# Scattering the experts' outputs in two passes of rounded fp32

## The chip, the cores and the metric

One Trainium2 chip, one of its cores. The metric is device time in microseconds (us) of one execution, median of three runs. TensorE is PE in the profile, VectorE is DVE, ScalarE is ACT, SyncE issues the DMAs of the weights (its queue is SPq). "fp32r" is rounded fp32: a matmul on it is one record in the trace, where a full fp32 matmul is two.

## The reference

Two layers of a hybrid backbone on 256 latent tokens (and 256 context tokens in the first layer) of width 1024. The change lies in the last stage alone, the channel mixer of layer 1, which is a top-2-of-8 mixture of SwiGLU experts:

```
def moe_swiglu(h, router, w1, w3, w2):
    logits = (h @ router).astype(jnp.float32)
    top_v, top_i = lax.top_k(logits, TOP_K)
    wts = jax.nn.softmax(top_v, axis=-1)
    comb = jnp.sum(jax.nn.one_hot(top_i, N_EXPERTS, dtype=jnp.float32) * wts[..., None], axis=-2)
    return sum(comb[..., e:e + 1].astype(h.dtype) * swiglu(h, w1[e], w3[e], w2[e])
               for e in range(N_EXPERTS))
...
        x = x + g2 * channel_mixer(h2, layer, ffn_w1, ffn_w3, ffn_w2, moe_router, moe_w1, moe_w3, moe_w2)
```

Eight experts, each with w1 and w3 of 1024x3584 and w2 of 3584x1024, all fp32. The result is the latent stream (256 x 1024).

## The kernel before, in words

All engines run programs written out by hand, with semaphores between them. Matmuls on weights use a split: a value is rounded to fp32r ("high"), the rest is kept as another fp32r ("low"), and three products (high x high, low x high, high x low) are added in PSUM.

**The expert stage.** Each expert has 128 slots. DVE ranks the tokens of each expert and writes 0/1 matrices Pm (token x slot) by comparing the rank with an iota (`select`, L1616). PE gathers: `gather` (L754 to L762) multiplies the tokens htok by Pm in full fp32. The expert's width of 3584 is worked in 14 pairs of 256 columns (PAIRS = 14). For each pair PE runs `up` (24 matmuls, 512 columns, L805 to L807), `turned` (2 transposes, L814) and `down` (12 matmuls, L826 to L828), which adds into banks 4 and 5 over the 14 pairs. ACT makes the high parts of the weights (L921, L927, L934), the silu (L1129) and the high part of the activation (L1133). DVE makes the low parts (L1269, L1275, L1282), the product (L1652) and the low part of the activation (L1656). SyncE fetches 3 pieces of 1 MB for each pair, each once the DVE instruction that reads the buffer's old contents is done.

**Scatter before.** Once, in the first expert: `select_rest` on DVE writes Pm for experts 1 to 7 and multiplies it by the token weights COMB into Pw (L1633). PE transposes Pw, 16 blocks of 128x128, in two halves (`turn_weighted`, L771 to L781, after `turned` of pair 1 and of pair 2). ACT copies them to the context half of xT (`keep_weighted`, L1112), which has no other use by then. For each expert e, at pairs 2 and 3 of the expert after it: ACT copies the sums from banks 4 and 5 to ysum (`sums`, L1124 and L1125). PE runs `scatter(e, half)`, at pair 2 with half 0 and at pair 3 with half 1, each 4 full-fp32 matmuls of 128x128 on 256 columns (L791), and DVE adds them to x with the gate (`update`, L1645, 4 instructions a half). The semaphore sums_read releases both the scatter and the next `down` that starts banks 4 and 5 anew. The last expert's scatter comes at the end, with nothing behind it but the updates and the output's DMA.

**Order around the change.** In each of an expert's pairs DVE runs: product of the pair before, act_low and down_low of the pair two before, up_b_low of the next, up_a_low of the one after, and at j = 2 and 3 `update`. PE at j = 2 runs up, turned, scatter half 0, down. At j = 3 it runs up, turned, scatter half 1, down.

Of the kernel before, what the change touches and what calls it, by code (L numbers as in the profile page):

```python
# [13 lines left out]
F32 = mybir.dt.float32  # L14
F32R = mybir.dt.float32r
# [5 lines left out]
P = 128  # L21
# [30 lines left out]
ALL_PAIRS = E * PAIRS  # L52
PIECE = 2 * D

BEFORE = {"ffn_y_free": 1, "scatter_free": 1, "up_a_used": 2, "moe_up_full": 2, "down_used": 2, "sums_read": 1}

# [65 lines left out]
def build(nc, xT_in, consts_in, pool_in, vec_in, cond_in, rows_in, router_in, first_in, mod_in, attn_in, ffn13_in, ffn2_in, moe_up_in, moe_down_in, out):  # L124
    with ExitStack() as ctx:
# [16 lines left out]
        def at(name, shape, off=None, dt=F32, parts=P):  # L142
# [5 lines left out]
            assert off + n <= room - 32, (name, off + n, room)  # L148
            return nc.alloc_sbuf_tensor_at(name, [parts, *shape], dt, offset=base + 4 * off)

        xT = at("xT", [KD, T])
        const = at("const", [CONST_LEN])
        vec = at("vec", [DEPTH, VEC_LEN])
# [99 lines left out]
        mprod = at("mprod", [2, 2 * P])  # L253
        mah = at("mact_high", [2, 2 * P], dt=F32R)
        mal = at("mact_low", [2, 2 * P], dt=F32R)
        Pw = at("Pw", [2, E, SLOTS], late)
        ysum = sg[:, :, :].rearrange("p a b -> p (a b)")

        banks = [ctx.enter_context(nc.psum_tensor(f"bank{b}", [P, 512], F32)) for b in range(8)]

# [187 lines left out]
        def _(pe):  # L448
# [315 lines left out]
            def experts(n):  # L764
# [6 lines left out]
                def turn_weighted(half):  # L771

                    if half == 0:
                        pe.wait_ge(S("weighted_ready"), n + 1)
                    else:
                        pe.wait_ge(S("turned_read"), 4 * n + 2)
                    for r in range(2 * half, 2 * half + 2):
                        for i in range(4):
                            e, t = divmod(4 * r + i, 2)
                            last = pe.transpose(banks[6 + r % 2][:, i * P:(i + 1) * P], Pw[:, t, e, :], C("ident"))  # L780
                        last.then_inc(S("turned_full"), 1)  # L781

                def scatter(e, half):

                    if half == 0:
                        pe.wait_ge(S("sums_read"), e + (n * E + 2))
                    for q in range(2 * half, 2 * half + 2):
                        pe.wait_ge(S("scatter_free"), e * 4 + (n * 4 * E + 1 + max(0, q - 1)))
                        for i in range(2):
                            k = 2 * q + i  # L790
                            last = mm(banks[6 + q % 2][:, i * LAT:(i + 1) * LAT], ysum[:, k * P:(k + 1) * P],  # L791
                                      xT[:, bass.ds(e, 1), LAT:T], start=True, stop=True)
                        last.then_inc(S("scatter_full"), 1)

                def up(g, u):
# [35 lines left out]
                def expert(e, first=False):  # L831
                    g0 = e * PAIRS + n * ALL_PAIRS
                    pe.wait_ge(S("gathered_low"), e * 2 + (n * 2 * (E + 1) + 2))
                    up(g0, 0)
                    if not first:
                        turned(g0 - 1, 1)
                        down(g0 - 2, 0)
                    up(g0 + 1, 1)
                    turned(g0, 0)
                    if not first:  # L840
                        down(g0 - 1, 1, stop=True)
                    up(g0 + 2, 0)
                    turned(g0 + 1, 1)
                    if first:
                        turn_weighted(0)
                    else:
                        scatter(e - 1, 0)
                    pe.wait_ge(S("sums_read"), e + (n * E + 1))
                    down(g0, 0, start=True)
                    up(g0 + 3, 1)  # L850
                    turned(g0 + 2, 0)
                    if first:
                        turn_weighted(1)
                    else:
                        scatter(e - 1, 1)
                    down(g0 + 1, 1)
                    with pe.Fori(2, PAIRS // 2 - 1) as q:
                        for u in range(2):
                            g = g0 + q * 2
                            up(g + u, u)  # L860
                            turned(g + (u - 1), 1 - u)
                            down(g + (u - 2), u)
                    g = g0 + (PAIRS - 2)
                    up(g, 0)
                    turned(g - 1, 1)
                    down(g - 2, 0)
                    up(g + 1, 1)
                    if first:
                        pe.wait_ge(S("turned_read"), 4 * n + 4)
                    pe.wait_ge(S("scatter_free"), e * 4 + (n * 4 * E + 1))  # L870
                    gather(e * SLOTS + SLOTS)
                    turned(g, 0)
                    down(g - 1, 1)
# [23 lines left out]
        def _(act):  # L897
# [210 lines left out]
            def experts(n):  # L1108
                def keep_weighted(half):
                    for r in range(2 * half, 2 * half + 2):  # L1110
                        act.wait_ge(S("turned_full"), n * 4 + r + 1)
                        fn(xT[:, 2 * r:2 * r + 2, LAT:T], banks[6 + r % 2][:, :].rearrange("p (e t) -> p e t", t=LAT), ACT.Copy) \  # L1112
                            .then_inc(S("turned_read"), 1)

                if n:
# [5 lines left out]
                def sums(e):  # L1121

                    act.wait_ge(S("down_used"), e * 2 * PAIRS + (2 * n * ALL_PAIRS + 2 * PAIRS + 2))
                    fn(ysum[:, 0:512], banks[4][:, :], ACT.Copy)  # L1124
                    fn(ysum[:, 512:D], banks[5][:, :], ACT.Copy).then_inc(S("sums_read"), 1)  # L1125

                def silu(g, u):
                    act.wait_ge(S("moe_up_full"), g + 3)
# [61 lines left out]
        def _(dve):  # L1190
# [417 lines left out]
            def experts(n):  # L1608
# [19 lines left out]
                def select_rest():  # L1628

                    for t in range(2):  # L1630
                        step(select(t, 1, E))
                        comb = R[:, COMB, t].unsqueeze(2).broadcast_to([P, E, SLOTS])
                        last = tt(Pw[:, t], Pm[:, t, 0:E * SLOTS].rearrange("p (e s) -> p e s", s=SLOTS), comb, ALU.mult)  # L1633
                    last.then_inc(S("weighted_ready"), 1)

                def update(e, half):

                    if half == 0:
                        dve.wait_ge(S("scatter_free"), e * 4 + (n * 4 * E + 1))
                    for q in range(2 * half, 2 * half + 2):  # L1640
                        dve.wait_ge(S("scatter_full"), e * 4 + (n * 4 * E + q + 1))
                        for i in range(2):
                            k = 2 * q + i
                            x = xT[:, k, 0:LAT]
                            last = stt(out=x, in0=banks[6 + q % 2][:, i * LAT:(i + 1) * LAT],  # L1645
                                       scalar=modT[:, 1, 5 * KD + k, 0:1], in1=x, op0=ALU.mult, op1=ALU.add)
                        last.then_inc(S("scatter_free"), 1)

                def product(g, u):

# [8 lines left out]
                def expert(e, first=False, last=False):  # L1659
                    g0 = e * PAIRS + n * ALL_PAIRS  # L1660
                    for j in range(4):
                        g, u = g0 + j, j % 2
                        if j or not first:
                            product(g - 1, 1 - u)
                        if j >= 2 or not first:
                            act_low(g - 2, u)
                            down_low(g - 2, u)
                        if first and j == 1:
                            select_rest()
                        up_b_low(g + 1, 1 - u)  # L1670
                        up_a_low(g + 2, u)
                        if j >= 2 and not first:
                            update(e - 1, j - 2)
                    with dve.Fori(2, PAIRS // 2 - 1) as q:
                        for u in range(2):
                            g = g0 + q * 2
                            product(g + (u - 1), 1 - u)
                            act_low(g + (u - 2), u)
                            down_low(g + (u - 2), u)
                            up_b_low(g + (u + 1), 1 - u)  # L1680
                            up_a_low(g + (u + 2), u)
                    for j in range(PAIRS - 2, PAIRS):
                        g, u = g0 + j, j % 2
                        product(g - 1, 1 - u)
                        act_low(g - 2, u)
                        down_low(g - 2, u)
                        if not last or j + 1 < PAIRS:
                            up_b_low(g + 1, 1 - u)
                        if not last:
                            up_a_low(g + 2, u)  # L1690
                    gathered_low(e * 2 + (n * 2 * (E + 1) + 2))
# [8 lines left out]
                down_low(g - 2, 0)  # L1700
                act_low(g - 1, 1)
                down_low(g - 1, 1)
                for half in range(2):
                    update(E - 1, half)

# [156 lines left out]
```

## Time and profile before

| what | value |
|---|---|
| time, median of 3 runs | 2235.92 us (2235.74 to 2236.14) |
| the profiled execution's own time | 2234.71 us |
| its span in the trace | 2232.9 us |
| PE busy | 2135.7 us, 96% of the span |
| DVE busy | 1713.1 us, 77% |
| ACT busy | 1120.7 us, 50% |
| DMA, mean over the span | 229 GB/s |

The profiled execution's time is its span and 1.8 us around it. Durations in the rows are those of single instructions; PE's overlap, so what one costs there is the step from one start to the next, which the chain of waits shows.

### The profile page before, as it was taken

The numbers are of one execution on the slowest core, as the hardware profiler recorded it, in microseconds if no ns is written. First come the engines' busy times: TensorE is split into PE (matmuls) and PEld (weight loads), VectorE is DVE, ScalarE is ACT, GpSimd is POOL, SyncE is SP. The second block draws the span as 40 slices with busy tenths as digits, with TensorE's granted clock in tenths as the row PEclk, the third lists the DMA queues.
The fourth block names the chain that finished last, engine by engine and source line by source line (L and its number), as shares of the span: only waits on it lengthen the run. The fifth ranks groups of instructions, "written<-read, shape, count | busy, mean of one in ns | idle before, by whom it ended". The sixth has DMA issues, their size and how long they took to land.

```text
span 2232.9 us, 27842 instructions
## 1 busy us (share of the span) xinstructions
PE 2135.7 (96%) x9866; PEld 1710.4 (77%) x9866; DVE 1713.1 (77%) x2158; ACT 1120.7 (50%) x1276; POOL 42.5 (2%) x84
## 2 busy tenths in 40 slices
PE   8989999998999999779997999999999999999997
PEld 6765776655788888667987888888888888888886
DVE  7777687646767766777745988988898988889895
ACT  3316221213333332434334777767777777767774
POOL 0000000000000000000000000000000000000000
PEclk9999999999999999899997999999999999999999
DMA  7500244343444443222444899989899999989993
GB/s 316 198 24 1 95 175 141 123 151 113 154 166 170 159 159 133 94 72 78 177 165 188 348 368 346 371 329 371 333 362 359 350 349 350 372 324 368 336 375 118
DMA packets 77284, 512.38 MB, mean 229 GB/s; under 512 B 8738, under 2 KB 9890, under 8 KB 22820
## 3 DMA queue, kind: packets, MB, share of 16 engines
q1 hardware_dynamic: 65700, 469.59, 55.9%
q0 software_dynamic: 11520, 41.95, 5.4%
q8 instruction: 38, 0.62, 0.1%
q14 instruction: 26, 0.21, 0.0%
HBM read 510.46 MB, written 1.05 MB: 229 GB/s over the span
## 4 chain that ended last, share of the span: by engine, by line
PE 88%; DVE 8%; ACT 2%; issue 2%; DMA 1%; SPq 0%; DVEq 0%; ACTq 0%
PE bank L807 9%; PE bank L805 9%; PE bank L806 9%; PE bank L556 5%; PE bank L558 5%; PE bank L557 5%; PE bank L668 5%; PE bank L826 5%; PE bank L828 5%; PE bank L827 5%; PE bank L678 4%; PE bank L724 2%; PE bank L725 2%; PE bank L726 2%; PE bank L700 2%; PE bank L710 2%
## 5 line engine op out<-in xcount | busy, mean ns | idle before, releaser
L934 ACT ACTIVATE down_high<-W 128x1024 fp32r<-128x1024 f32 x224 | 237.1, 1064 | 139.3 <-PE bank L828 139.2
L1275 DVE TENSOR_TENSOR up_b_low<-W,up_b_high 128x2048 fp32r<-128x2048 f32 x112 | 256.5, 2290 | 56.5 <-ACT up_b_high L927 56.5
L1282 DVE TENSOR_TENSOR down_low<-W,down_high 128x1024 fp32r<-128x1024 f32 x224 | 271.8, 1223 | 31.8 <-ACT down_high L934 22.5
L556 PE MATMUL bank<-h_high,tile_high 128*128 128x512 f32 (+1 forms) x704 | 259.7, 369 | 11.7 <-DVE tile_low L1326 11.7
L1269 DVE TENSOR_TENSOR up_a_low<-W,up_a_high 128x2048 fp32r<-128x2048 f32 x112 | 255.8, 2284 | 1.9 <-ACT up_a_high L921 1.9
L558 PE MATMUL bank<-h_high,tile_low 128*128 128x512 f32 (+1 forms) x704 | 239.3, 340 | 0.0
L557 PE MATMUL bank<-h_low,tile_high 128*128 128x512 f32 (+1 forms) x704 | 239.2, 340 | 0.0
L921 ACT ACTIVATE up_a_high<-W 128x2048 fp32r<-128x2048 f32 x112 | 212.9, 1901 | 2.1 <-PE bank L807 2.1
L927 ACT ACTIVATE up_b_high<-W 128x2048 fp32r<-128x2048 f32 x112 | 213.2, 1903 | 0.0
L826 PE MATMUL bank<-down_high,mact_high 128*128 128x512 f32 x448 | 186.4, 416 | 2.6 <-DVE down_low L1282 2.6
L828 PE MATMUL bank<-down_low,mact_high 128*128 128x512 f32 x448 | 176.3, 393 | 0.0
L805 PE MATMUL bank<-up_a_high,gathered_high 128*128 128x512 f32 x448 | 174.5, 390 | 1.4 <-DVE gathered_low L1603 1.4
L827 PE MATMUL bank<-down_high,mact_low 128*128 128x512 f32 x448 | 175.4, 392 | 0.0
L807 PE MATMUL bank<-up_b_low,gathered_high 128*128 128x512 f32 x448 | 175.0, 391 | 0.0
L805 PE MATMUL bank<-up_b_high,gathered_high 128*128 128x512 f32 x448 | 174.4, 389 | 0.3 <-DVE up_b_low L1275 0.3
L807 PE MATMUL bank<-up_a_low,gathered_high 128*128 128x512 f32 x448 | 174.3, 389 | 0.0
L806 PE MATMUL bank<-up_b_high,gathered_low 128*128 128x512 f32 x448 | 174.3, 389 | 0.0
L806 PE MATMUL bank<-up_a_high,gathered_low 128*128 128x512 f32 x448 | 174.3, 389 | 0.0
L556 PEld LDWEIGHTS bank<-h_high,tile_high 128*128 128x128 f32 x704 | 135.6, 193 | 35.2 <-DVE tile_low L1326 12.6
L1065 ACT ACTIVATE sg<-bank 128x512 f32<-128x512 f32 (+1 forms) x64 | 31.4, 490 | 261.2 <-PE bank L558 261.1
L557 PEld LDWEIGHTS bank<-h_low,tile_high 128*128 128x128 f32 x704 | 135.7, 193 | 21.9 <-issue 7.9
L558 PEld LDWEIGHTS bank<-h_high,tile_low 128*128 128x128 f32 x704 | 135.5, 192 | 14.7
(229 smaller groups left out, 4087.7 us busy)
## 6 DMA issues: line engine op xcount, KB each, us to landing
W<-in_moe_up SPq DMA_DIRECT2D x224, 1024.0 KB, 6.0
W<-in_moe_down SPq DMA_DIRECT2D x112, 1024.0 KB, 4.9
W<-in_w_mod_later POOLq DMA_DIRECT2D x80, 512.0 KB, 3.7
W<-in_ffn SPq DMA_DIRECT2D x33, 1024.0 KB, 4.8
W<-in_attn_blocks SPq DMA_DIRECT2D x24, 1280.0 KB, 5.9
W<-in_attn_blocks SPq DMA_DIRECT2D x22, 1024.0 KB, 5.2
W<-in_attn_blocks SPq DMA_DIRECT2D x8, 1536.0 KB, 7.1
shift_tiles<-in_w_mod_first SPq DMA_DIRECT2D x8, 512.0 KB, 13.9
```

Source lines behind the costliest of these rows:

```text
L556: mm(b[:, 0:n], wh[:, r, k, :], hh[:, k, 0:n], start=k == 0, stop=False)
L557: mm(b[:, 0:n], wh[:, r, k, :], hl[:, k, 0:n], start=False, stop=False)
L558: last = mm(b[:, 0:n], wl[:, r, k, :], hh[:, k, 0:n], start=False, stop=k == KD - 1)
L805: mm(b[:, :], hgh[:, k, :], high[u][:, kk, :], start=k == 0, stop=False)
L806: mm(b[:, :], hgl[:, k, :], high[u][:, kk, :], start=False, stop=False)
L807: last = mm(b[:, :], hgh[:, k, :], low[u][:, kk, :], start=False, stop=k == KD - 1)
L826: mm(b[:, :], mah[:, u, a], ch[:, h, w], start=start and h == 0, stop=False, skip_group_check=True)
L827: mm(b[:, :], mal[:, u, a], ch[:, h, w], start=False, stop=False, skip_group_check=True)
L828: last = mm(b[:, :], mah[:, u, a], cl[:, h, w], start=False, stop=stop and h == 1, skip_group_check=True)
L1269: tt(al[u][:], raw_a[u].rearrange("p (k n) -> p k n", k=KD // 2), ah[u][:].bitcast(F32), ALU.subtract) \
L1275: tt(bl[u][:], raw_b[u].rearrange("p (k n) -> p k n", k=KD // 2), bh[u][:].bitcast(F32), ALU.subtract) \
L1282: tt(cl[:, h, :], raw_c[u][:, h * D:(h + 1) * D], ch[:, h, :].bitcast(F32), ALU.subtract) \
```

## The change

The token weights leave the scatter matrix. What PE transposes and ACT keeps is now the 0/1 matrix Pm, kept as fp32r (PmT, at xT's address). The weight of each slot, one number for each slot and expert, is made once by 16 matmuls of Pm with one column of COMB (in `turn_weighted(0)`, into bank 7), and DVE copies it to wslot after `down_low` of pair 0, at j = 2 of the first expert; PE's transposes of r = 1 into the same bank wait for that copy. The sums of an expert are multiplied by wslot as they leave PSUM: ACT writes the high part (ysh, with a scale operand of one value a partition), and DVE, in a new function `sums_low`, the low part (ysl), before act_low at j = 2. The scatter is two fp32r matmuls on the same PSUM region instead of one full-fp32 matmul. The multiplication of Pm by COMB on DVE is gone. sums_low_ready, counted by DVE, takes the place of sums_read, counted by ACT. The gather stays as it was.

```
-        Pw = at("Pw", [2, E, SLOTS], late)
-        ysum = sg[:, :, :].rearrange("p a b -> p (a b)")
+        ysh = at("sums_high", [D], late, dt=F32R)
+        ysl = at("sums_low", [D], late + D, dt=F32R)
+        PmT = at("PmT", [KD, T], xT_at, dt=F32R)
+        wslot = sg[:, 0, 0:E]
...
                 def turn_weighted(half):
                     if half == 0:
-                        pe.wait_ge(S("weighted_ready"), n + 1)
+                        pe.wait_ge(S("rest_selected"), n + 1)
+                        for e in range(E):
+                            for t in range(2):
+                                last = mm(banks[7][:, e:e + 1], Pm[:, t, e * SLOTS:(e + 1) * SLOTS],
+                                          R[:, COMB, t, e:e + 1], start=t == 0, stop=t == 1)
+                        last.then_inc(S("slot_weights_full"), 1)
                     else:
                         pe.wait_ge(S("turned_read"), 4 * n + 2)
                     for r in range(2 * half, 2 * half + 2):
+                        if r == 1:
+                            pe.wait_ge(S("slot_weights_read"), n + 1)
                         for i in range(4):
                             e, t = divmod(4 * r + i, 2)
-                            last = pe.transpose(banks[6 + r % 2][:, i * P:(i + 1) * P], Pw[:, t, e, :], C("ident"))
+                            last = pe.transpose(banks[6 + r % 2][:, i * P:(i + 1) * P],
+                                                Pm[:, t, e * SLOTS:(e + 1) * SLOTS], C("ident"))
...
                 def scatter(e, half):
                     if half == 0:
-                        pe.wait_ge(S("sums_read"), e + (n * E + 2))
+                        pe.wait_ge(S("sums_low_ready"), e + (n * E + 2))
...
-                            last = mm(banks[6 + q % 2][:, i * LAT:(i + 1) * LAT], ysum[:, k * P:(k + 1) * P],
-                                      xT[:, bass.ds(e, 1), LAT:T], start=True, stop=True)
+                            b = banks[6 + q % 2][:, i * LAT:(i + 1) * LAT]
+                            mm(b, ysh[:, k * P:(k + 1) * P], PmT[:, bass.ds(e, 1), LAT:T], start=True, stop=False)
+                            last = mm(b, ysl[:, k * P:(k + 1) * P], PmT[:, bass.ds(e, 1), LAT:T], start=False, stop=True)
...
-                    pe.wait_ge(S("sums_read"), e + (n * E + 1))
+                    pe.wait_ge(S("sums_low_ready"), e + (n * E + 1))
                     down(g0, 0, start=True)
...
-                    fn(ysum[:, 0:512], banks[4][:, :], ACT.Copy)
-                    fn(ysum[:, 512:D], banks[5][:, :], ACT.Copy).then_inc(S("sums_read"), 1)
+                    for hf in range(2):
+                        fn(ysh[:, hf * 512:(hf + 1) * 512], banks[4 + hf][:, :], ACT.Copy, scale=wslot[:, bass.ds(e, 1)]) \
+                            .then_inc(S("sums_high_ready"), 1)
...
                 def select_rest():
                     for t in range(2):
-                        step(select(t, 1, E))
-                        comb = R[:, COMB, t].unsqueeze(2).broadcast_to([P, E, SLOTS])
-                        last = tt(Pw[:, t], Pm[:, t, 0:E * SLOTS].rearrange("p (e s) -> p e s", s=SLOTS), comb, ALU.mult)
-                    last.then_inc(S("weighted_ready"), 1)
+                        last = select(t, 1, E)
+                    last.then_inc(S("rest_selected"), 1)
...
+                def sums_low(e):
+                    for hf in range(2):
+                        dve.wait_ge(S("sums_high_ready"), e * 2 + (2 * n * E + hf + 1))
+                        a = slice(hf * 512, (hf + 1) * 512)
+                        last = stt(out=ysl[:, a], in0=banks[4 + hf][:, :], scalar=wslot[:, bass.ds(e, 1)], in1=ysh[:, a].bitcast(F32),
+                                   op0=ALU.mult, op1=ALU.subtract)
+                    last.then_inc(S("sums_low_ready"), 1)
...
                         if j >= 2 or not first:
+                            if j == 2 and not first:
+                                sums_low(e - 1)
                             act_low(g - 2, u)
                             down_low(g - 2, u)
                         if first and j == 1:
                             select_rest()
+                        if j == 2 and first:
+                            dve.wait_ge(S("slot_weights_full"), n + 1)
+                            dve.tensor_copy(wslot, banks[7][:, 0:E]).then_inc(S("slot_weights_read"), 1)
...
                 act_low(g - 1, 1)
                 down_low(g - 1, 1)
+                sums_low(E - 1)
                 for half in range(2):
                     update(E - 1, half)
```

## Rows read from the trace of the kernel before

**Rows 1.** The page: the span in 40 slices, PE busy in tenths, and its granted clock.
```profile
PE   8989999998999999779997999999999999999997
...
PEclk9999999999999999899997999999999999999999
```

**Rows 2.** Who waited for whom from 1260 to 2200: us in total, times, longest.
```profile
DVE up_b_low L1275 <- ACT up_b_high L927: 51.8, 96, 0.6
```

**Rows 3.** The chain of waits at one expert's boundary: start us, us, what.
```profile
1358.42 0.22 PE bank L814 x2
1358.63 1.73 PE bank L791 x8
1360.36 0.24 PE bank L826
...
1378.94 0.24 PE bank L826
```

**Rows 4.** The chain of waits in layer 1's projections, rounded fp32 on 256 columns.
```profile
1062.11 0.12 PE bank L558
```

**Rows 5.** Timeline of DVE at the boundary: start, us, tile, count, idle before.
```profile
1354.40 0.42 DVE L1656 TENSOR_TENSOR mact_low<-bank,mact_high 128x256 fp32r<-128x256 f32 x1 [2.10 <-ACT mact_high L1133]
1355.35 2.36 DVE L1282 TENSOR_TENSOR down_low<-W,down_high 128x1024 fp32r<-128x1024 f32 x2 [0.52 <-ACT down_high L934]
1358.10 2.29 DVE L1275 TENSOR_TENSOR up_b_low<-W,up_b_high 128x2048 fp32r<-128x2048 f32 x1 [0.39 <-ACT up_b_high L927]
...
1373.65 2.35 DVE L1282 TENSOR_TENSOR down_low<-W,down_high 128x1024 fp32r<-128x1024 f32 x2
```

**Rows 6.** Timeline of ACT there.
```profile
1353.50 0.59 ACT L1125 ACTIVATE sg<-bank 128x512 f32<-128x512 f32 x1
```

**Rows 7.** Groups of DVE and ACT by shape: count, busy us, mean ns, idle before.
```profile
L1445 DVE SCALAR_TENSOR_TENSOR conv<-ypad,vec,conv 128x512 f32<-128x512 f32 x60 | 41.7, 745 | 0.0
...
L1065 ACT ACTIVATE sg<-bank 128x512 f32<-128x512 f32 x32 | 19.1, 597 | 184.3 <-PE bank L558 184.3
...
L967 ACT ACTIVATE root<-bank,const 128x512 f32<-128x512 f32 x3 | 2.1, 687 | 11.3 <-PE bank L475 11.3
```

**Rows 8.** Two stretches, PE alone: length, busy (records), clock, DMA share, GB/s.
```profile
36.00:38.00 2.00, 2.00 (x20) 1.00 0.96 404
1205.40:1207.70 2.30, 2.26 (x10) 0.50 0.00 0
```

**Rows 9.** Timeline of DVE in the first expert, pairs 1 and 2.
```profile
1225.36 1.22 DVE L1633 TENSOR_TENSOR Pw<-Pm,R 128x1024 f32<-128x1024 f32 x1
...
1228.76 2.29 DVE L1275 TENSOR_TENSOR up_b_low<-W,up_b_high 128x2048 fp32r<-128x2048 f32 x1
...
1233.83 2.35 DVE L1282 TENSOR_TENSOR down_low<-W,down_high 128x1024 fp32r<-128x1024 f32 x2
```

**Rows 10.** Timeline of PE there: start, us, tile, idle before and its releaser.
```profile
1230.42 0.39 PE L807 MATMUL bank<-up_a_low,gathered_high 128*128 128x512 f32 x1
...
1231.10 0.50 PE L805 MATMUL bank<-up_b_high,gathered_high 128*128 128x512 f32 x1 [0.30 <-DVE up_b_low L1275]
```

**Rows 11.** The chain of waits, in the first expert and at the end.
```profile
1234.39 0.87 PE bank L780 x8
...
2219.84 0.48 ACT sg L1124
...
2220.98 1.15 PE bank L791 x4
```

**Rows 12.** Timeline of DVE at the end.
```profile
2222.22 1.67 DVE L1645 SCALAR_TENSOR_TENSOR xT<-bank,modT,xT 128x256 f32<-128x256 f32 x4 [4.23 <-PE bank L791]
2224.32 1.74 DVE L1645 SCALAR_TENSOR_TENSOR xT<-bank,modT,xT 128x256 f32<-128x256 f32 x4 [0.43 <-PE bank L791]
```

**Rows 13.** SyncE's queue from 1230 to 2200, and all DMA from 1260 to 1340.
```profile
SPq L404 <- DVE down_low L1282: 350.7, 109, 8.1
...
DMA packets 4184, 30.44 MB, mean 381 GB/s; under 512 B 469, under 2 KB 469, under 8 KB 469
```

More of the change, by code:

```diff
@@ L53 @@
 PIECE = 2 * D
-BEFORE = {"ffn_y_free": 1, "scatter_free": 1, "up_a_used": 2, "moe_up_full": 2, "down_used": 2, "sums_read": 1}
+BEFORE = {"ffn_y_free": 1, "scatter_free": 1, "up_a_used": 2, "moe_up_full": 2, "down_used": 2, "sums_low_ready": 1}
 COLS = {}
@@ L149, in at @@
             return nc.alloc_sbuf_tensor_at(name, [parts, *shape], dt, offset=base + 4 * off)
+        xT_at = top[0]
         xT = at("xT", [KD, T])
@@ L1111, in keep_weighted @@
                         act.wait_ge(S("turned_full"), n * 4 + r + 1)
-                        fn(xT[:, 2 * r:2 * r + 2, LAT:T], banks[6 + r % 2][:, :].rearrange("p (e t) -> p e t", t=LAT), ACT.Copy) \
+                        fn(PmT[:, 2 * r:2 * r + 2, LAT:T], banks[6 + r % 2][:, :].rearrange("p (e t) -> p e t", t=LAT), ACT.Copy) \
                             .then_inc(S("turned_read"), 1)
```

## The prediction

> **What bounds the kernel now.** I read the page's slices first: in the last half of the span, the expert stage, PE is busy in nine tenths or more of every slice and its granted clock stays at full speed [rows 1]. Then the waits of that stage: DVE waits 51.8 us for ACT, 96 times, at most 0.6 us each, and PE does not stand among the waiters at all [rows 2]. Last the chain of waits at one expert's boundary, where every piece is PE's [rows 3]. So between the first expert and the last one the time is the sum of PE's steps. What the change takes from PE there is worth its full length, so long as the wait that would come last next (DVE's low parts) still comes before PE. Two places are different: the first expert's early pairs, where DVE is once in the chain, and the end, where PE, ACT and DVE take turns. I take the three places one after the other, against the profiled execution (2234.71 us, of which the span is 2232.9); the median of the runs is 1.2 us above it, and the difference is carried over to the median.
>
> **Scatter on PE, experts 0 to 6 (inside the loop).** A half is 4 full-fp32 matmuls, 8 records, and takes 1.73 us of the chain [rows 3], 0.433 us a matmul. After the change it is 8 fp32r matmuls of 128x128 on 256 columns. The trace has the same shape in layer 1's projections, each with its own stationary tile too, and there the chain steps 0.12 us [rows 4]. So a half is 8 x 0.12 = 0.96 us, 0.77 us less, and 7 experts x 2 halves save 10.8 us. Bounds: at the smallest step that a 128-column record shows, 0.109 us (0.87 us for 8) [rows 11], it would be 12.0 us; at the step of today's records, 0.216 us, nothing. I take 0.12, since shape, type and change of the stationary tile are the same.
>
> **ACT's and DVE's new work at the boundary.** ACT's two copies get a scale operand. The nearest pair of rows, 128x512 without and with a one-value-a-partition operand, is 597 and 687 ns [rows 7]: +0.09 us each, 0.18 us an expert, in front of ACT's next work. DVE gets two 128x512 instructions of scalar_tensor_tensor form, 745 ns each [rows 7], 0.66 us from start to start because neighbours overlap by some 0.08: 1.4 us an expert. They stand between product and act_low at j = 2. Today DVE is idle there for 2.10 us, waiting for ACT's mact_high, which ACT makes only after its two copies [rows 5, 6]. ACT's second copy runs 1353.50 to 1354.09, and the first starts 0.49 us ahead of it; with the dearer form the first ends about 1353.70. DVE's two run 1353.75 to 1355.15, act_low follows to 1355.5, and down_low, which starts at 1355.35 today, starts at about 1355.5. Then up_b_low waits for ACT as before and moves only with ACT's 0.2 us (1358.10 to 1358.3). So the idle stretch hides nearly all of it. Behind the new wait on DVE's queue stand act_low, down_low, up_b_low, up_a_low and the updates, and SyncE's three pieces, which follow the low parts.
>
> Does PE still find its operands? The scatter's half 0 starts at 1358.63 [rows 3] and needs the second DVE instruction, done at 1355.15: 3.5 us to spare. The closest one is down of pair 2. PE starts it at 1378.94 today [rows 3], both halves of the scatter earlier that is 1.54 us sooner, 1377.4. Its down_low runs 1373.65 to 1376.0 [rows 5] and moves by 0.2 us, because DVE works without a gap from 1358.10 up to it. That leaves 1.2 us (2.7 today), and beyond it ACT, released earlier by PE, gives DVE its inputs earlier as well, so the lead grows again. I cost the DVE and ACT part at nothing. Without the 2.10 us of cover PE would lose up to 0.2 + 1.4 - 1.2 = 0.4 us an expert, 2.8 us in all.
>
> **The first expert.** Removed: the two products of Pm with COMB, 1.22 us each, and the waits between; they stand ahead of up_b_low (start 1228.76) [rows 9]. PE waits for that up_b_low: its last ready matmul ends its step at 1230.42 + 0.23 = 1230.65 and the next starts at 1231.10 [rows 10]. With up_b_low 2.4 us earlier this goes: -0.45 us. The rest of the 2.4 us gives DVE a lead and no more.
> Added on PE: 8 experts x 2 = 16 matmuls of one column, full fp32, 32 records, ahead of the 8 transposes of the half, between turned and down, so on the path. The nearest row is L489, the same form with two columns and a fresh stationary tile each: 20 records in 2.00 us at full clock, 0.100 us a record [rows 8]. 32 x 0.100 = +3.2 us. Bounds: one record a matmul, 1.6 us; the step of L748 to L752 (8 columns), 2.26 us for 10 records, but at half the clock [rows 8], 7.2 us. I take 3.2, as PE has been at full clock for over 15 us by then.
> The transposes themselves stay (8 in 0.87 us [rows 11]). New is that those of r = 1 wait for DVE's copy, which stands behind down_low of pair 0. That down_low ends at 1236.2 today (1233.83 + 2.35) [rows 9] and 2.4 us sooner after, 1233.8, while the 16 matmuls end only about 1237.0. The copy is made while PE runs the 4 transposes of r = 0 (0.44 us), so the wait is at most 0.05 us. Its other queue, DVE's up_b_low of pair 3, waits for ACT's keep_weighted today too, and all of that moves with PE. First expert together: 3.2 - 0.45 + 0.05 = +2.8 us.
>
> A rule of the Trainium skill speaks for a smaller price here. Its page "VectorE: DVE Perf Modes", in the section on the TRN2 errata, gives a matmul max(60, 6 + columns) cycles at 2.4 GHz, which for one column is 25 ns, and an estimate from it is 32 x 0.025 = 0.8 us in place of 3.2. For 256 columns the same rule gives 0.109 us where [rows 4] has 0.12. The two-column row of this trace, 0.100 us, disagrees with the rule at narrow matmuls, so the sum goes by the row.
>
> **The end.** Today: ACT 2219.84, PE's scatter 2220.98, DVE's first update 2222.22, last one over at 2224.32 + 1.74 = 2226.06 [rows 11, 12]. After: ACT's first copy ends 2220.53, DVE's two instructions run 2220.58 to 2221.99, the scatter starts 2222.05 (+1.07 us). The first 4 fp32r matmuls take 0.48 us where 4 records took 0.87, and the update follows 0.37 us behind them as today (2222.22 less 2220.98 and 0.87): 2222.90. From there DVE is the slower one, 4 instructions in 1.67 us. Bank 6 comes free after two of them, at 2223.77, and the second half's first update follows 0.05 + 0.85 us behind, at 2224.7, and ends at 2226.4. So +0.3 us: the new hop costs 1.07 and the shorter matmuls give 0.8 back.
>
> **Sum.** -10.8 + 2.8 + 0.3 = -7.7 us, 2227.0 for the profiled execution and 2228.2 for the median. With the bounds of the column matmuls alone it is -9.3 to -3.7, and with the scatter's step at its lower bound too, -10.5: 2225.4 to 2232.2.
>
> **The rivals.**
> 1. The narrow matmuls are nearly free, priced by columns and not by the load of the stationary tile. Place: turn_weighted(0). For it: they write one column. Against it: [rows 8]. At a quarter of the row's step the first expert is +0.4 us: -10.1, 2225.8. The rule named above says the same. Chance 0.07.
> 2. The scatter on PE gets no shorter, since fp32r pairs that change the stationary tile and add into one region step as today's records do, or PE's saved time comes back as waits for weights. Against the first: [rows 4]. For the second: DMA moves 381 GB/s in the loop. Against it: SyncE waits for DVE, up to 8.1 us at a time, before it issues, and so is not the late one [rows 13]. Then nothing is saved: +2.8 and +1.07 at the end, +3.9, 2239.8. Chance 0.06.
> 3. DVE becomes part of the bound at each boundary, as its 1.4 us are not covered: 2.8 us lost, or up to 5 with ACT's register work ahead of it: -4.9 to -2.7, 2231.0 to 2233.2. Chance 0.08.
> 4. The other side: the low sums come so late that PE stands at down of pair 2. All of DVE's queue would have to be more than 1.2 us later than I have it. It makes the kernel slower by over 0.2% if it is 1.2 + (7.7 + 4.5) / 7 = 2.9 us late an expert; at 4 us late it is 7 x 2.8 = 19.6 us, +11.9, 2247.8. For it: DVE works without a gap for two pairs there. Against it: 2.10 us of idle just ahead of the new work. Chance 0.04.
> My forecast has the remaining 0.75, with a range of its own of 2226.5 to 2231.0.
>
> **How the numbers follow.** A measurement of this kernel can tell about 0.2%, 4.5 us, from no change. Faster by more than that means below 2231.45. The forecast is there but for its upper bound on the narrow matmuls, which I give 0.02; rival 1 is there, and of rival 3 about 0.02. That is 0.73 + 0.07 + 0.02 = 0.82 faster. Slower is rival 4 and a sliver of rival 2, 0.05. The rest, 0.13, is within. The range 2225.2 to 2232.6 takes in both bounds, rival 1 and part of rival 3, and leaves out rivals 2 and 4.
>
> **What would show each step right or wrong.** In the chain: a scatter half of 0.96 us (x8) in place of 1.73, and 2 to 3.5 us of the 32 new records before the transposes in the first expert. In the timeline of DVE: the two instructions of sums_low at 745 ns inside the old gap of 2.10 us, act_low behind them with no idle. In the waits from 1260 to 2200: still no PE row. At the end: the scatter a good microsecond later after the last down, the last update about 0.3 us later. The prediction is wrong if PE shows waits for down_low at pair 2, if the step of the fp32r pairs is not 0.12, or if the one-column matmuls step far from 0.100 us.

## The result, and the profile after

The changed kernel takes 2228.86 us (median of 9 runs, 2226.42 to 2230.06) against 2235.74 us of the kernel before on the same chips: a ratio of 0.9969, with a 95% interval of 0.9959 to 0.9978. That is 6.9 us less. The forecast was 7.7 us less, 2228.2.

The profiled execution's span is 2227.1 us, 5.8 less than before. The times at which each expert's sums leave PSUM cut the stage into places that can be compared. Timeline of ACT, the first, second, seventh and last such instruction in the changed kernel:

```profile
1358.57 1.27 ACT L1137 ACTIVATE sums_high<-bank,sg 128x512 fp32r<-128x512 f32 x2 [2.71 <-PE bank L840]
1481.98 1.27 ACT L1137 ACTIVATE sums_high<-bank,sg 128x512 fp32r<-128x512 f32 x2 [2.71 <-PE bank L840]
...
2098.91 1.27 ACT L1137 ACTIVATE sums_high<-bank,sg 128x512 fp32r<-128x512 f32 x2 [2.61 <-PE bank L840]
2213.82 1.27 ACT L1137 ACTIVATE sums_high<-bank,sg 128x512 fp32r<-128x512 f32 x2 [3.13 <-PE bank L840]
```

The same in the kernel before:

```profile
1353.01 0.60 ACT L1124 ACTIVATE sg<-bank 128x512 f32<-128x512 f32 x1 [2.61 <-PE bank L828]
1478.06 0.60 ACT L1124 ACTIVATE sg<-bank 128x512 f32<-128x512 f32 x1 [2.61 <-PE bank L828]
...
2103.33 0.60 ACT L1124 ACTIVATE sg<-bank 128x512 f32<-128x512 f32 x1 [2.61 <-PE bank L828]
```

From one expert to the next it is 125.05 us before and 123.41 after. From the first to the last sums (2219.84 before [rows 11]) it is 866.83 and 855.25 us. Together with the starts of the stage's first `up` (1216.62 before, 1217.83 after) and the end of the last update the difference of the spans comes apart like this:

| place | before, us | after, us | difference | forecast |
|---|---|---|---|---|
| up to the first `up` of expert 0 | 1216.62 | 1217.83 | +1.21 | 0 |
| from there to the first sums | 136.39 | 140.74 | +4.35 | +2.8 |
| first to last sums, seven scatters | 866.83 | 855.25 | -11.58 | -10.8 |
| last sums to the end of the last update | 6.22 | 6.40 | +0.18 | +0.3 |
| rest of the span | 6.84 | 6.88 | +0.04 | 0 |

The first line is no effect of the change: the two programs are the same up to there. It is mostly the first gather, which runs from one clock level into the other; over the twelve profiled executions of this study the way from its start to the first `up` took 7.0 us in five and 7.8 to 7.9 us in seven, and which of the two it was did not follow what the kernels changed later.

**The scatter.** The chain of waits at the boundary that answers to [rows 3], a half of the scatter being eight pieces between L826 and L838:

```profile
1363.88 0.22 PE bank L826 x2
1364.10 0.12 PE bank L803
1364.22 0.12 PE bank L804
...
1364.92 0.12 PE bank L804
1365.04 0.23 PE bank L838
```

It takes 0.94 us where it took 1.73. DVE there, the answer to [rows 5]:

```profile
1357.34 0.42 DVE L1672 TENSOR_TENSOR mprod<-msil,bank 128x256 f32<-128x256 f32 x1
1359.40 1.41 DVE L1665 SCALAR_TENSOR_TENSOR sums_low<-bank,sg,sums_high 128x512 fp32r<-128x512 f32 x2 [1.64 <-ACT sums_high L1137]
1360.72 0.41 DVE L1676 TENSOR_TENSOR mact_low<-bank,mact_high 128x256 fp32r<-128x256 f32 x1
1361.10 2.36 DVE L1295 TENSOR_TENSOR down_low<-W,down_high 128x1024 fp32r<-128x1024 f32 x2
1363.84 2.29 DVE L1288 TENSOR_TENSOR up_b_low<-W,up_b_high 128x2048 fp32r<-128x2048 f32 x1 [0.39 <-ACT up_b_high L939]
```

The two new instructions stand in the stretch that was idle. From ACT's first sums instruction (1358.57) to up_b_low it is 5.27 us; before it was 1358.10 - 1353.01 = 5.09. So everything behind moves by the 0.18 us of ACT's two scale operands and by nothing else. The groups by shape have the two prices, ACT's at 685 ns and DVE's at 746:

```profile
L1137 ACT ACTIVATE sums_high<-bank,sg 128x512 fp32r<-128x512 f32 x16 | 10.2, 685 | 22.0 <-PE bank L840 22.0
L1665 DVE SCALAR_TENSOR_TENSOR sums_low<-bank,sg,sums_high 128x512 fp32r<-128x512 f32 x16 | 11.3, 746 | 13.9 <-ACT sums_high L1137 13.9
```

In the list of waits from 1260 to 2200 there is still no row in which PE is the one who waits.

**The first expert.** Here is what the forecast did not have. The chain of waits, and behind it the timeline of PE at the same place:

```profile
1234.96 3.47 PE bank L780 x32
1238.42 0.93 PE bank L790 x8
```

```profile
1239.46 0.63 PE L839 MATMUL bank<-down_high,mact_low 128*128 128x512 f32 x1
1239.89 0.63 PE L840 MATMUL bank<-down_low,mact_high 128*128 128x512 f32 x1
1240.32 0.63 PE L838 MATMUL bank<-down_high,mact_high 128*128 128x512 f32 x1
...
1242.84 0.39 PE L838 MATMUL bank<-down_high,mact_high 128*128 128x512 f32 x1
1243.07 0.39 PE L839 MATMUL bank<-down_high,mact_low 128*128 128x512 f32 x1
```

The 32 records of the one-column matmuls take 3.47 us, 0.108 each. But behind them `down` steps 0.43 us from start to start for some eight matmuls, and then 0.23. PE alone by stretches (length, busy and records, granted clock, DMA):

```profile
1236.00:1238.00 2.00, 2.00 (x20) 1.00 1.01 369
1238.00:1240.00 2.00, 2.00 (x15) 0.84 0.63 246
1240.00:1242.00 2.00, 2.00 (x6) 0.50 0.02 8
1242.00:1244.00 2.00, 2.00 (x9) 0.80 0.00 0
```

PE is busy in all of it and does not wait, and yet the granted clock goes from 2.4 to 1.2 GHz. By the chain of waits this `down` takes 4.32 us, from 1239.36 to the next `up` at 1243.68.

### The profile page after: what moved, and what is told of

It is laid out like the page before. It is cut to its first block, busy times and chain, and to the rows that moved or that the text cites. A ratio compares the mean times of both kernels' runs of the same rounds, so it can differ in the third digit from the quotient of the medians.

```text
span 2227.1 us, 27945 instructions
## 1 busy us (share of the span) xinstructions
PE 2130.5 (96%) x9898; PEld 1710.0 (77%) x9898; DVE 1717.4 (77%) x2173; ACT 1122.3 (50%) x1276; POOL 42.5 (2%) x84
## 4 chain that ended last, share of the span: by engine, by line
PE 88%; DVE 7%; ACT 2%; issue 2%; DMA 1%; SPq 0%; DVEq 0%; ACTq 0%
PE bank L819 9%; PE bank L817 9%; PE bank L818 9%; PE bank L559 5%; PE bank L561 5%; PE bank L560 5%; PE bank L671 5%; PE bank L838 5%; PE bank L840 5%; PE bank L839 5%; PE bank L681 4%; PE bank L727 2%; PE bank L728 2%; PE bank L729 2%; PE bank L712 2%; PE bank L702 2%
## 5 line engine op out<-in xcount | busy, mean ns | idle before, releaser
L838 PE MATMUL bank<-down_high,mact_high 128*128 128x512 f32 x448 | 184.1, 411 | 2.6 <-DVE down_low L1295 2.6
```

The source lines that it names most:

```text
L838: mm(b[:, :], mah[:, u, a], ch[:, h, w], start=start and h == 0, stop=False, skip_group_check=True)
```

## The experiments

Three questions were open. Is the fall of the clock the one-column matmuls' doing, or this execution's? Is the scatter's step all that the loop gained? And how much cover does DVE have at the boundary? Ratios are to the kernel before, timed beside each one.

**The changed kernel again** (no edit).

> The changed kernel once more, beside the other three. Theory A (the 16 one-column matmuls leave PE's granted clock at half for a while right behind them): the clock falls to 0.50 in the first down behind them in this execution as well, and about 9 of its 12 matmuls step 0.43 us instead of 0.23. Theory B (the fall was this one execution's, by chance): full clock there. Ratio to the kernel before 0.997 either way.

Ratio 0.9968 (0.9956 to 0.9980), 2228.33 us. The fall is there again: the 32 records take 3.47 us, `down` behind them steps 0.43, and from 1240 to 1242 the granted clock is 0.50. From the first `up` to the first sums it is 140.80 us (140.74). The three other kernels below that keep these 16 matmuls as they are (full_fp32_scatter, low_twice, low_thrice) show it too: with the first profile it is five executions of five. Theory B, chance, falls.

**The same number of matmuls with 64 columns.**

```
-    last = mm(banks[7][:, e:e + 1], Pm[:, t, e * SLOTS:(e + 1) * SLOTS],
-              R[:, COMB, t, e:e + 1], start=t == 0, stop=t == 1)
+    last = mm(banks[7][:, 64 * e:64 * e + 64], Pm[:, t, e * SLOTS:(e + 1) * SLOTS],
+              R[:, COMB, t, e:e + 1].broadcast_to([P, 64]), start=t == 0, stop=t == 1)
...
-    dve.tensor_copy(wslot, banks[7][:, 0:E])
+    dve.tensor_copy(wslot, banks[7][:, 0:512:64])
```

> The slot weights' 16 matmuls write 64 equal columns each instead of one; the records stay 32. Theory A (too little work in the array): the step stays near 0.108 us (3.5 us in all), the clock stays at 1.0 behind them, the down behind them takes 2.75 us instead of 4.6, and the time is some 1.9 us below the changed kernel's. Theory B (chance), or a fall that comes from stationary loads or full fp32 as such: no change in the fall, the same time.

Ratio 0.9962 (0.9949 to 0.9976), 2227.12 us. PE by stretches and the chain:

```profile
1238.00:1240.00 2.00, 2.00 (x13) 1.00 0.13 53
1240.00:1242.00 2.00, 2.00 (x10) 1.00 0.00 0
```

```profile
1234.10 3.52 PE bank L780 x32
```

The records take 3.52 us, as long as with one column, and the clock stays at full speed behind them. From the first `up` to the first sums it is 139.14 us, 1.60 less than in the changed kernel. That is the price of the fall, read directly; the forecast of this run had 1.9, since it took the slow `down` at 4.6 us, where the chain has 4.32, and 2.74 here. A fall that comes from the stationary loads or from full fp32 as such is out too: both are the same here. This is one execution against five. The median is 1.2 us below that of `again`, beside which it ran, and the two intervals overlap; the timing alone could not have told it from no change.

**The slot weights' matmuls left out.** All slot weights are 1 then, so the experts' outputs are added unweighted and the result is not the reference's.

```
-    for e in range(E):
-        for t in range(2):
-            last = mm(banks[7][:, e:e + 1], Pm[...], R[:, COMB, t, e:e + 1], ...)
-    last.then_inc(S("slot_weights_full"), 1)
...
-    dve.wait_ge(S("slot_weights_full"), n + 1)
-    dve.tensor_copy(wslot, banks[7][:, 0:E]).then_inc(S("slot_weights_read"), 1)
+    dve.memset(wslot, 1.0).then_inc(S("slot_weights_read"), 1)
```

> The 16 matmuls are left out (the slot weights are all set to 1, so the experts' outputs are added unweighted). Theory A: 3.5 us of steps, the wait for DVE's copy and 1.9 us of half clock go, 5 to 5.5 us below the changed kernel, 0.9945 of the one before. Theory B: 3.5 us below, 0.9954.

Ratio 0.9945 (0.9931 to 0.9958), 2223.11 us, 5.2 us below `again`. From the first `up` to the first sums 135.66 us: 5.08 below the changed kernel, which is the 3.47 of the records and the 1.60 of the clock, so the wait for DVE's copy costs nothing that can be seen. (In this kernel the second four transposes wait for a memset at the copy's place; in the changed kernel they follow the first four at the usual step of 0.11 us.) It is also 0.73 below the kernel before. That is what the removed products of Pm and COMB give, for which the forecast had 0.45. The rest is in the chain of waits of the kernel before, at the place where PE waited for up_b_low:

```profile
1231.10 0.50 PE bank L805
1231.61 0.24 PE bank L806
```

PE stood still for 0.45 us there, and the first matmul behind the wait then took 0.51 us to the next one where 0.23 is usual, another 0.28: together 0.73. The forecast counted the standstill alone.

**The slot weights in rounded fp32.** Pm is written as fp32r, and the gather and the transposes read the same bits as fp32.

```
+    step(dve.tensor_copy(comb_hl[:, :, :, 0], R[:, COMB]))
+    step(tt(comb_hl[:, :, :, 1], R[:, COMB], comb_hl[:, :, :, 0].bitcast(F32), ALU.subtract))
...
-    last = mm(banks[7][:, e:e + 1], Pm[:, t, e * SLOTS:(e + 1) * SLOTS], R[:, COMB, t, e:e + 1], ...)
+    last = mm(banks[7][:, 2 * e:2 * e + 2], Pm[:, t, e * SLOTS:(e + 1) * SLOTS], comb_hl[:, t, e, :], ...)
...
-    dve.tensor_copy(wslot, banks[7][:, 0:E])
+    dve.tensor_reduce(wslot, banks[7][:, 0:2 * E].rearrange("p (e h) -> p e h", h=2), AX, ALU.add)
```

> The slot weights in fp32r: Pm and the high and low parts of the weights as two columns, one record a matmul, 16 instead of 32; DVE adds the two columns. If a narrow matmul costs its stationary load a record: 16 x 0.108 = 1.7 us instead of 3.5, and with half the time of narrow work the clock falls less or not: 1.8 to 3.7 us below the changed kernel. If fp32r with few columns is slow, the step is 0.2 us or more and nothing is gained.

Ratio 0.9951 (0.9937 to 0.9965), 2224.10 us, 4.2 us below `again`. The chain of waits and PE by stretches behind it:

```profile
1233.48 1.68 PE bank L781 x16
1235.16 0.95 PE bank L791 x8
```

```profile
1236.00:1238.00 2.00, 2.00 (x11) 1.00 0.90 373
1238.00:1240.00 2.00, 2.00 (x10) 1.00 0.11 45
```

16 records in 1.68 us, 0.105 each, and the clock stays up. The expectation's other case, a step of 0.2 us or more, did not come. From the first `up` to the first sums it is 137.37 us, 3.37 less than in the changed kernel: 1.79 from the records and 1.6 from the clock.

**That kernel again, and with each half released for itself.** In the second one sums_low counts after each of its two instructions, and each half of the scatter waits for its own.

```
-                    if half == 0:
-                        pe.wait_ge(S("sums_low_ready"), e + (n * E + 2))
+                    pe.wait_ge(S("sums_low_ready"), e * 2 + (2 * n * E + 2 + half))
...
-                    pe.wait_ge(S("sums_low_ready"), e + (n * E + 1))
+                    pe.wait_ge(S("sums_low_ready"), e * 2 + (2 * n * E + 1))
...
-                    last.then_inc(S("sums_low_ready"), 1)
+                        last.then_inc(S("sums_low_ready"), 1)
```

> The kernel of slots_rounded once more, beside half_release on the same chip: 16 records of about 0.108 us, no fall of the clock behind them, 0.9951 of the kernel before within 0.001. If the clock that stayed up in its first look was chance, it falls here.

> The kernel of slots_rounded, with sums_low releasing each half of the scatter for itself (half 0 reads only the first 512 sums). In the loop nothing, as PE comes to the scatter some 3 us after the sums are ready. At the end the scatter starts one DVE instruction (0.66 us) sooner, and the last update ends 0.3 to 0.7 us sooner after the last down: 6.39 us becomes 5.7 to 6.1, if the clock is the same. Against the kernel before 0.995; the difference to slots_rounded is under what the timing can tell, so the trace decides.

Again: 0.9953 (0.9940 to 0.9967), 2224.86 us, 16 records in 1.68 us, no fall behind them. With the halves released apart: 0.9951 (0.9938 to 0.9965), 2224.47 us; the period is the same 123.41 us, and from the last sums to the end of the last update it is 5.81 us where `rounded_again` has 6.40. The trace shows the 0.6 us; the times cannot tell the two kernels apart.

**The scatter back in full fp32**, all else as in the changed kernel: ACT writes the scaled sums whole, as fp32, and keeps Pm as fp32. DVE still makes the low part, but nothing reads it.

```
-    mm(b, ysh[:, k * P:(k + 1) * P], PmT[:, bass.ds(e, 1), LAT:T], start=True, stop=False)
-    last = mm(b, ysl[:, k * P:(k + 1) * P], PmT[:, bass.ds(e, 1), LAT:T], start=False, stop=True)
+    last = mm(b, ysum[:, k * P:(k + 1) * P], xT[:, bass.ds(e, 1), LAT:T], start=True, stop=True)
```

> The changed kernel with the scatter back in one full-fp32 matmul for each 128 rows (the low part of the sums is still made by DVE and not used; ACT writes the scaled sums whole). If PE's step in the scatter is what was saved inside the loop: an expert's period goes from 123.41 back to 125.05 us, 11.5 us for seven, and the time is some 4.5 us above the kernel before (1.002). If something else in the change shortened the loop (the new order of waits), the period stays below 125.

Ratio 1.0026 (1.0016 to 1.0036), 2240.71 us. The period is back at 125.05 us, to the hundredth. So all of the gain in the loop comes from the scatter's matmuls. The time is 5.9 us above the kernel before, where 4.5 were expected: the first expert keeps its 4.4 us, and from the last sums to the end of the last update it is 8.52 us in place of 6.22. Of these 2.3 us some 1.1 are the hop over DVE, which no shorter matmul gives back here; the rest lies from the scatter's start on, where the granted clock was lower:

```profile
2225.00:2227.00 2.00, 2.00 (x6) 0.50 0.02 4
```

The expectation names neither.

**The two-pass scatter alone.** The token weights stay in Pw, rounded to fp32r as ACT keeps it; there are no slot weights and no scale operands, and DVE's low part is a plain subtraction.

```
+    comb = R[:, COMB, t].unsqueeze(2).broadcast_to([P, E, SLOTS])
+    last = tt(Pw[:, t], Pm[:, t, 0:E * SLOTS].rearrange("p (e s) -> p e s", s=SLOTS), comb, ALU.mult)
...
-    last = pe.transpose(banks[6 + r % 2][:, i * P:(i + 1) * P], Pm[:, t, e * SLOTS:(e + 1) * SLOTS], C("ident"))
+    last = pe.transpose(banks[6 + r % 2][:, i * P:(i + 1) * P], Pw[:, t, e, :], C("ident"))
```

> The two-pass scatter alone: token weights stay in the matrix as before (rounded to fp32r there, so they lose their low bits), no slot weights, no scale operands. Expected: period 123.4 us, first expert as in the kernel before, the end +0.1 us: 11.4 us below the kernel before, 0.9949. If the scale operands or the copy for the slot weights cost time in the loop, it is below that.

Ratio 0.9947 (0.9933 to 0.9960), 2223.59 us. The period is 123.41 us without the scale operands too (ACT's copies take 596 ns here, 685 with the operand), and from the first `up` to the first sums it is 136.35 us, as in the kernel before (136.39). So the part of the change that is not the scatter's two passes costs 4.4 us in the first expert and nothing in the loop; what it keeps is the precision of the token weights.

**DVE's new work doubled and tripled.** The extra instructions have the same operands and write memory that nothing reads.

```
     last = stt(out=ysl[:, a], in0=banks[4 + hf][:, :], ...)
+    for more in (unused areas)[0:1 or 0:2]:
+        last = stt(out=more, in0=banks[4 + hf][:, :], scalar=wslot[:, bass.ds(e, 1)], in1=ysh[:, a].bitcast(F32), ...)
```

> sums_low's two instructions are four (the extra ones write unused memory): +1.3 us on DVE an expert. In the changed kernel down_low of pair 2 is done some 1.0 us before PE needs it. Cover theory: 0.3 us lost an expert, 2 us in all. If the margin is larger than that: nothing in the loop, 0.7 us at the end. If DVE's time counts in full: 9 us.

> Six instructions: +2.6 us on DVE an expert. Cover theory: 1.6 us lost an expert (2.6 less the 1.0 of margin), period 125.0, PE waits for down_low at pair 2, 11 us in the loop and 1.3 at the end. If ACT and DVE recover part elsewhere it is less, never more than 18.

Doubled: 0.9972 (0.9960 to 0.9984), 2228.78 us, and the period is 123.41 us, unchanged. Tripled: 0.9992 (0.9983 to 1.0002), 2233.39 us, the period is 123.67, 0.26 us longer, and no more. The cover theory had 0.3 and 1.6 us an expert, so both runs miss its numbers, in the same direction. The end was missed the other way: from the last sums to the end of the last update it is 8.27 us and 10.07, where 6.40 and the expected 0.7 and 1.3 make 7.1 and 7.7. DVE's extra instructions lie there in full, 1.3 and 2.6 us, and the granted clock was at 0.50 in the doubled kernel's second half of the scatter and in the whole of the tripled one's. The timelines of DVE and of PE in the tripled one show where the margin ends in the loop:

```profile
1360.43 1.40 DVE L1668 SCALAR_TENSOR_TENSOR const<-bank,sg,sums_high 128x512 f32<-128x512 f32 x2
1361.75 0.41 DVE L1679 TENSOR_TENSOR mact_low<-bank,mact_high 128x256 fp32r<-128x256 f32 x1
1362.08 2.35 DVE L1295 TENSOR_TENSOR down_low<-W,down_high 128x1024 fp32r<-128x1024 f32 x2
...
1379.89 2.35 DVE L1295 TENSOR_TENSOR down_low<-W,down_high 128x1024 fp32r<-128x1024 f32 x2
```

```profile
1363.15 0.28 PE L804 MATMUL bank<-PmT,sums_low 128*128 x1
1363.35 0.50 PE L838 MATMUL bank<-down_high,mact_high 128*128 128x512 f32 x1
1363.69 0.39 PE L839 MATMUL bank<-down_high,mact_low 128*128 128x512 f32 x1
...
1380.98 0.38 PE L826 MATMUL bank<-const,mprod 128*128 128x128 f32 x2
1381.16 0.50 PE L838 MATMUL bank<-down_high,mact_high 128*128 128x512 f32 x1
```

The rows merge the two instructions of a down_low; one of them takes 1.22 us. So the first half of down_low of pair 0 ends at 1362.08 + 1.22 = 1363.30, and PE's `down` of pair 0 starts at 1363.35, 0.20 us behind the scatter's last record (0.12 in the doubled kernel), and then needs 0.34 us to the next (0.22 there). That is 0.20 of the 0.26 us. The other 0.06 lies at pair 2: the first half of down_low ends at 1379.89 + 1.22 = 1381.11, and PE's `down` starts at 1381.16, 0.18 us behind the first transpose (0.14 in the doubled kernel), with 0.34 us to the next (0.32 there). So in both places PE starts 0.05 us behind the first half; the second is needed six matmuls later and is never waited for. The profile writes no releaser there, so that it is this half that PE waits for is read from the times; that DVE's work is the cause is shown, as nothing else differs from the doubled kernel. From the end of the first half to PE's start of `down` it is, in us:

| kernel | pair 0 | pair 2 |
|---|---|---|
| changed | 2.56 | 1.90 |
| doubled | 1.29 | 1.12 |
| tripled | 0.05 | 0.05 |

## Why the prediction was right, and where it was not

**The scatter's step** was right in kind and nearly in size: 7 x 2 x 0.77 = 10.8 forecast, 11.58 measured, 1.65 an expert in place of 1.54. The first half takes 0.94 us and the second 0.92, not 0.96, which gives 0.4 us of the 0.8. The rest lies right behind them: `down` takes 2.72 and 2.74 us there where it took 2.75 and 2.76 (1360.36 to 1363.11 and 1370.51 to 1373.27 before, 1365.04 to 1367.76 and 1374.35 to 1377.09 after). That `down` steps so because of the scatter ahead of it was not tried apart, but full_fp32_scatter shows that nothing else in the change moves the period. Rival 2, no shorter scatter or no gain from it, is out.

**ACT's and DVE's work at nothing** was right, and for the reason given: the idle stretch takes it in, and all behind it moves by 0.18 us. The margin was mis-sized, though. The prediction had 1.2 us at down of pair 2, counting to the end of both halves of down_low. PE starts on the first half alone, and from its end to PE's start there are 1.90 us in the changed kernel (0.8 from the end of the second), so doubling DVE's new work, 1.3 us more, cost nothing in the loop. With the work tripled, pair 0, behind the scatter, and pair 2 run out together. Rival 3, new work that is not covered, and rival 4, low parts that come too late, are out: the period fell by the whole of the scatter's gain, and in low_twice it still did.

**The first expert** is where the sum was off: +2.8 forecast, +4.35 measured. Term by term: the 32 records 3.47 for 3.2 (0.108 a record, not the 0.100 of L489); the wait for DVE's copy nothing for 0.05; the removed products -0.73 for -0.45, as the slow first matmul behind the standstill goes with them; and 1.60 us of half clock behind the one-column matmuls, for which there was no term. The prediction took PE's clock as given because PE had been at full speed for over 15 us and would have no gap. wide_columns takes the narrowness away at the same number and length of records, and the 1.60 us go. Rival 1, nearly free narrow matmuls, would have moved this place the other way and is out: the price is the same for 1 and 64 columns.

The Trainium skill has a rule on the load of the stationary tile: the page "TensorE: Matmul & The Clock Gate", in its section on LDWEIGHTS, puts it at the number of columns / 1.2 ns, and an estimate from it for 128 columns is 107 ns. The steps here, 0.108 and 0.105 us, agree with it. That the load sets the step is argued from this; the runs show that the columns do not. The rule of the Trainium skill's page "VectorE: DVE Perf Modes" that the prediction quotes, by which a matmul of one column would be 25 ns, does not hold here.

The fall of the clock could have been read before the change, at the very rows of the price. In seven of the twelve profiled executions, that of the kernel before among them, PE was at full clock for most of the last 32 records of L489, full fp32 with two columns. In all seven the clock was back at 1.2 GHz between 38.70 and 39.84 us, within 0.51 us of the start of the last of these records. In three of them (no_slot_matmuls, rounded_again, low_twice) records were still to come, so there at least it was not PE's idle time behind them. PE by stretches in the kernel before, where the clock falls within the stretch, and in rounded_again:

```profile
38.80:39.20 0.40, 0.40 (x5) 0.93 1.09 443
```

```profile
36.50:38.50 2.00, 2.00 (x20) 1.00 0.98 400
38.80:39.20 0.40, 0.40 (x4) 0.50 1.06 426
```

**The end** came as worked out, +0.18 for +0.3, when the clock stays up. The chain of waits:

```profile
2213.82 0.70 ACT sums_high L1137
...
2214.54 1.42 DVE sums_low L1665 x2
...
2216.00 0.38 PE bank L803
...
2216.85 0.89 DVE xT L1656 x2
```

**Together** the loop gave 0.8 us more than forecast and the first expert 1.55 less, and the median, 6.9 us less instead of 7.7, is nearer than either. That it is so near is luck in part: the two errors have opposite signs.

## What to carry to other kernels

Where PE never waits, a matmul's step read from the same shape elsewhere in the trace is what a change of its type is worth; count the loop's repetitions, then look at what is done once. A run of matmuls with one column each, each with its own stationary tile, costs 0.108 us a record here, as much as with 64 columns, and after them possibly the clock of what follows: give them more columns if the time is the same anyway, or make them fewer. Look what the clock did behind the row that the price comes from. A margin ends at the first operand that the waiting engine needs, not at the last one of the group.

## What the runs showed of the hardware

The granted clock can fall while PE is busy without a gap. It fell from 2.4 to 1.2 GHz behind the narrow matmuls in all five executions with 32 records of one column (3.47 us), in none of the one with 32 records of 64 columns (3.52 us), and in none of the three with 16 records of two columns (1.68 us). The 32 full-fp32 records of two columns in L489 were followed by a fall too, in all seven executions in which PE was at full clock there, so two columns alone do not keep it up. Whether the smaller number of records or their type, fp32r, did it in the last ones was not tried apart.

At the end of the kernel PE stands still for over 2 us ahead of the last scatter, and there the clock varies with the execution: of the six whose kernels are the same from the last `down` on, with all of sums_low in front of the scatter, it stays up in four (after, again, slots_rounded, rounded_again) and is lower in the scatter in two (wide_columns, no_slot_matmuls). The stretches of wide_columns, to be held against full clock all through in the changed kernel's profiled execution:

```profile
2213.00:2215.00 2.00, 1.49 (x8) 0.68 0.01 4
2215.00:2217.00 2.00, 1.82 (x8) 0.50 0.02 4
```

From the last sums to the end of the last update that was 7.20 us instead of 6.40. In no_slot_matmuls it was 6.95. Such a fall, 0.6 to 0.8 us, and the two lengths of the first gather, some 0.8 us apart, belong to the execution, not to the kernel.
